# The expert loop of a two-block transformer kernel: spread rows, gather and turning in another order

## The reference, cut to what matters

```python
D_MODEL, N_EXPERTS, TOP_K, D_EXPERT = 1024, 32, 4, 1024
SWIGLU_LIMIT, SWIGLU_ALPHA = 7.0, 1.702

def _expert_ffn(xb, w_gu, b_gu, w_down, b_down):
    gu = xb @ w_gu + b_gu
    gate, up = gu[:, :D_EXPERT], gu[:, D_EXPERT:]
    gate = jnp.minimum(gate, SWIGLU_LIMIT)
    up = jnp.clip(up, -SWIGLU_LIMIT, SWIGLU_LIMIT)
    glu = gate * jax.nn.sigmoid(SWIGLU_ALPHA * gate)
    return ((up + 1.0) * glu) @ w_down + b_down

def moe(xf, router_w, router_b, w_gu, b_gu, w_down, b_down):
    logits = (xf @ router_w + router_b).astype(F32)
    top_val, top_idx = lax.top_k(logits, TOP_K)
    gate = jax.nn.softmax(top_val, axis=-1)
...
    ys = lax.map(run_block, (xs, block_e)).reshape(n_slots, -1)
    return jnp.zeros(xf.shape, F32).at[slot_tok].add(ys.astype(F32) * slot_w[:, None])
```

## Time and profile before

| | us |
|---|---|
| median of 3 runs | 3159.39 (3158.26 to 3159.98) |
| the profiled execution | 3160.19 |
| its span | 3158.3 |
| TensorE busy in the span | 2995.8 (95%) |
| VectorE, ScalarE busy | 842.7, 376.8 |
| share of the chain of waits on L302, all products with weights | 76% |
| the expert stage | from about 659 to 1627 |

### The profile page before, as it was taken

The page is one execution under the profiler, slowest core; times in us unless marked ns, Lnnn a source line. Parts: engine busy times, 40 slices in busy tenths (PEclk is TensorE's granted clock), DMA queues, the critical chain, the costliest instruction groups (busy, mean ns, idle before and its releaser), DMA issues.

```text
span 3158.3 us, 35752 instructions
## 1 busy us (share of the span) xinstructions
PE 2995.8 (95%) x14810; PEld 1952.2 (62%) x14811; DVE 842.7 (27%) x1939; ACT 376.8 (12%) x817; POOL 27.7 (1%) x55
## 2 busy tenths in 40 slices
PE   8989889989999999999989999999999999989999
PEld 6867678833333333333338886675788888756888
DVE  2536341222222222222232103543211111133210
ACT  2122230100000000000010001121000000012000
POOL 0000000000000000000000000000000000000000
PEclk9999999989999999999989999898999999986999
DMA  5122234459999999999963333220243334321340
GB/s 193 53 90 97 80 120 157 187 227 412 425 422 425 421 422 424 422 424 426 421 284 134 133 137 141 81 107 35 107 152 142 133 133 155 133 80 54 133 160 14
DMA packets 49501, 654.86 MB, mean 207 GB/s; under 512 B 5825, under 2 KB 8017, under 8 KB 10193
## 3 DMA queue, kind: packets, MB, share of 16 engines
q1 hardware_dynamic: 45248, 642.90, 51.1%
q0 software_dynamic: 3104, 9.32, 0.9%
q10 hardware_dynamic: 1040, 1.05, 0.1%
HBM read 652.19 MB, written 1.05 MB: 207 GB/s over the span
## 4 chain that ended last, share of the span: by engine, by line
PE 92%; DVE 4%; ACT 2%; issue 1%; DMA 1%; POOL 0%; PEldq 0%; DVEq 0%; PEld 0%; SPq 0%; ACTq 0%; POOLq 0%
PE bank L302 76%; PE bank L2070 2%; PE bank L1087 2%; PE bank L2042 2%; PE bank L2434 1%; PE bank L2443 1%; PE bank L2452 1%; DVE expert_x_slots L2174 1%; PE bank L2048 1%; ACT expert_y_slots L2116 1%; PE bank L2300 1%; PE bank L2838 1%; PE bank L1339 1%; PE bank L2853 0%; PE bank L733 0%
## 5 line engine op out<-in xcount | busy, mean ns | idle before, releaser
L302 PE MATMUL bank<-ffn_x_gained,weight_ring 128*128 128x272 f32 (+1 forms) x2816 | 641.0, 390 | 9.3 <-DVE ffn_x_gained L2317 9.3
L302 PEld LDWEIGHTS bank<-ffn_x_gained,weight_ring 128*128 128x128 f32 x2816 | 536.5, 191 | 112.6 <-DVE ffn_x_gained L2317 11.0
L302 PE MATMUL bank<-weight_ring,expert_x_slots_t 128*64 128x512 f32 x2048 | 457.6, 600 | 0.0
L302 PE MATMUL bank<-x,first_weight_ring 128*128 128x256 f32 x1376 | 323.3, 392 | 29.1 <-DMA first_weight_ring<-weight_stream 12.8
L302 PEld LDWEIGHTS bank<-weight_ring,expert_x_slots_t 128*64 128x64 f32 x2048 | 142.3, 138 | 312.5 <-issue 312.5
L302 PE MATMUL bank<-ffn_h,weight_ring 128*128 128x272 f32 (+1 forms) x1408 | 322.0, 389 | 2.1 <-DVE ffn_up L2396 2.1
L302 PEld LDWEIGHTS bank<-x,first_weight_ring 128*128 128x128 f32 x1376 | 266.4, 196 | 73.2 <-issue 23.9
L302 PEld LDWEIGHTS bank<-ffn_h,weight_ring 128*128 128x128 f32 x1408 | 267.2, 190 | 54.0 <-DVE ffn_up L2396 3.8
L302 PE MATMUL bank<-weight_ring,expert_hidden_slots_t 128*64 128x512 f32 x1024 | 226.8, 595 | 0.0
L302 PE MATMUL bank<-even_hn,weight_ring 128*128 128x272 f32 x656 | 163.9, 406 | 4.4 <-DVE even_hn L2334 4.4
L2179 DVE TENSOR_TENSOR moe_rows<-moe_rows,bank 128x512 f32<-128x512 f32 x128 | 79.4, 682 | 330.9 <-PE bank L2070 330.9
(11 more groups left out here) (572 smaller groups left out, 2374.9 us busy)
## 6 DMA issues: line engine op xcount, KB each, us to landing
weight_ring<-weight_stream SPq DMA_DIRECT2D x276, 2048.0 KB, 9.9
first_weight_ring<-weight_stream SPq DMA_DIRECT2D x30, 2048.0 KB, 7.7
x<-x_t SPq DMA_DIRECT2D x1, 1024.0 KB, 5.9
out_t<-x ACTq DMA_DIRECT2D x1, 1024.0 KB, 4.7
c_ret_ret_q<-const_ret_q POOLq DMA_DIRECT2D x1, 544.0 KB, 5.1
c_ret_ret_k<-const_ret_k POOLq DMA_DIRECT2D x1, 544.0 KB, 5.7
c_odd_pool_inv<-const_pool_inv POOLq DMA_DIRECT2D x1, 544.0 KB, 3.6
c_hgrn_hgrn_levels<-const_hgrn_levels POOLq DMA_DIRECT2D x1, 512.0 KB, 3.8
```

Of the source, the lines that this page charges most:

```text
L302: ins = K.nc.tensor.matmul(out, lhsT, rhs, start=start, stop=stop)
```

## The change

In the short path the spread rows are turned into bank 0 instead of bank 2, behind one more wait of TensorE, for VectorE's reading of the gate products (`gate_read`, a second reader of `gate_sb`). The gather is cut by halves of the tokens: the first half stays before the turning of the activations, the second goes behind it. The next tokens are turned behind the down products instead of before them, into bank 3, and ScalarE copies them to `xt` behind its copy of the down products instead of before. VectorE takes the spread rows from bank 0. In the long path the operations stay in their order, with the added wait.

```diff
+        gate_read = gate_sb.reader()
...
-            def gather_next(pe):
-
-                pe.wait_ge(*pick_ready.take())
-                for b in range(2):
-                    for g in range(2):
-                        ins = nc.tensor.matmul(bank[3][rows[g], :], pick[:, b, :], K.x_rows[:, b, g * HW:(g + 1) * HW], start=b == 0, stop=b == 1)
-                ins.then_inc(*gathered.post())
+            def gather_next(pe, b):
+
+                if b == 0:
+                    pe.wait_ge(*pick_ready.take())
+                for g in range(2):
+                    ins = nc.tensor.matmul(bank[3][rows[g], :], pick[:, b, :], K.x_rows[:, b, g * HW:(g + 1) * HW], start=b == 0, stop=b == 1)
+                if b == 1:
+                    ins.then_inc(*gathered.post())
...
                 pe.wait_ge(*spread_ready.take())
+                pe.wait_ge(*gate_read.take())
                 for b in range(2):
-                    nc.tensor.transpose(bank[2][:, b * P:(b + 1) * P], spread[:, b, :, :].rearrange("p a s -> p (a s)"), eye)
-                gather_next(pe)
+                    nc.tensor.transpose(bank[0][:, b * P:(b + 1) * P], spread[:, b, :, :].rearrange("p a s -> p (a s)"), eye)
+                gather_next(pe, 0)
                 pe.wait_ge(*h_ready.take())
                 for j in range(4):
                     ins = nc.tensor.transpose(bank[5][:, j * P:(j + 1) * P], h[:, 0, j * P:(j + 1) * P], eye)
                 ins.then_inc(*ht_ready.post())
-                turn_next(pe)
+                gather_next(pe, 1)
                 pe.wait_ge(*ht_sb.take())
                 few_linear(pe, bank[2], ht_few, None, y_ready)
+                turn_next(pe, 3)
                 pe.wait_ge(*ys_sb.take())
...
                 act.activation(flat(ht_few[:, :, :]), bank[5][:, :], ACT.Copy).then_inc(*ht_sb.post())
-                copy_next(act)
                 act.wait_ge(*y_ready.take())
                 act.activation(ys[:, :], bank[2][:, :], ACT.Copy).then_inc(*ys_sb.post())
+                copy_next(act, 3)
...
-                dve.tensor_copy(spread_t[:, :], bank[2][:, 0:T])
+                dve.tensor_copy(spread_t[:, :], bank[0][:, 0:T])
```

More of the change, by code:

```diff
@@ L2035, in _, with turn_next @@
             eye = K.con["eye"][:, :]
-            def gather_next(pe):
-                pe.wait_ge(*pick_ready.take())
-                for b in range(2):
-                    for g in range(2):
-                        ins = nc.tensor.matmul(bank[3][rows[g], :], pick[:, b, :], K.x_rows[:, b, g * HW:(g + 1) * HW], start=b == 0, stop=b == 1)
-                ins.then_inc(*gathered.post())
-            def turn_next(pe):
+            def gather_next(pe, b):
[5 more added lines that the diff above has]
+                    ins.then_inc(*gathered.post())
+            def turn_next(pe, at):
                 pe.wait_ge(*xs_sb.take())
                 for j in range(4):
-                    ins = nc.tensor.transpose(bank[4][:, j * P:(j + 1) * P], xs[:, j * P:(j + 1) * P], eye)
+                    ins = nc.tensor.transpose(bank[at][:, j * P:(j + 1) * P], xs[:, j * P:(j + 1) * P], eye)
                 ins.then_inc(*xt_ready.post())
@@ L2078, in many @@
                 many_linear(pe, 4, lambda k: K.x[:, k, 0:T], D, up_ready)
+                pe.wait_ge(*gate_read.take())
                 pe.wait_ge(*h_ready.take())
-                gather_next(pe)
-                turn_next(pe)
+                gather_next(pe, 0)
+                gather_next(pe, 1)
+                turn_next(pe, 4)
                 for b in range(2):
@@ L2089, in many @@
                 pe.nop().then_inc(*out_ready.post())
[L2091 removed]
+            taken = [(sel_ready, 1), (xs_sb, 1), (xt_sb, 1), (spread_ready, 1), (pick_ready, 1), (gate_read, 1), (h_ready, 1), (ht_sb, 1), (ys_sb, 1)]
             posted = [gathered, xt_ready, gate_ready, up_ready, ht_ready, y_ready, out_ready]
@@ L2104, in _, with copy_next @@
         def _(act):
-            def copy_next(act):
+            def copy_next(act, at):
                 act.wait_ge(*xt_ready.take())
-                act.activation(flat(xt[:, :, :]), bank[4][:, :], ACT.Copy).then_inc(*xt_sb.post())
+                act.activation(flat(xt[:, :, :]), bank[at][:, :], ACT.Copy).then_inc(*xt_sb.post())
             def few(act):
@@ L2120, in many @@
                 act.activation(flat(sg[:, :, :]), flat(gate[:, :, :]), ACT.Sigmoid, scale=1.702).then_inc(*sig_ready.post())
-                copy_next(act)
+                copy_next(act, 4)
                 act.wait_ge(*ht_ready.take())
```

## The result

| | us | ratio to before, 95% interval |
|---|---|---|
| before, 4 runs | 3159.68 | |
| changed, 4 runs | 3132.88 (3132.02 to 3137.22) | 0.9918 (0.9901 to 0.9935) |
| changed, once more, 4 runs | 3131.81 | 0.992 (0.9904 to 0.9937) |
| profiled execution, before and changed | 3160.19, 3133.48 | |

The change brings 26.8 us, 0.8%. The forecast was 14.0 us, 3145.4; the measured time lies a tenth of a microsecond under the range's low end of 3133.0. The direction and the saving on TensorE were right. The pace of the stream of weights, which limited the forecast, was wrong.

What follows compares the result with a forecast made beforehand. TensorE was taken as the bound, 29.76 us an expert against the weight stream's 29.70; stored lead 12.6, last expert 0.9 and earlier stream start 0.5 gave 14.0 us, so 3145.4 us, range 3133 to 3149.

Steps and rivals of the forecast that it cites:

- TensorE is the bound before, by a little: Expert stage: TensorE takes 29.76 us an expert, the weight stream 29.70, so TensorE bounds by 0.06 us per expert.
- 0.91 us saved on TensorE: New order from spread rows to output products: TensorE saves 0.91 us per expert, 0.56 at the lower bound, needing 28.85.
- The turning hidden in the wait for ScalarE, at 0: Next tokens turned behind the down products, inside the wait for ScalarE's copy: extra cost 0, upper bound 0.35 us.
- A full 0.53 for the added change: Rule against the sum: each change of shape costs 0.53 us; 0.38 of 0.91 us left, 12.2 of 14.0 in all.
- The stream needs 29.70 us an expert: Expert stage: the weight stream, working without pause, delivers an expert's weights in 29.70 us, at 423 GB/s.
- the lead: Time from an expert's fourth transfer landing to first use: 10.9 to 12.6 us, used up after 12 to 14 experts.
- Sum by the right figure: Whole-kernel gain: 12.6 us of stored lead, 0.9 in the last expert, 0.5 from the stream's earlier start: 14.0 us.
- The earlier start of the stream: Second and third expert's releases come up to 0.9 us sooner each: 0.5 us gained, bounds 0 and 2.
- The stream is faster than these rows say: Rival, expert stage: at 428 GB/s the gain is 22.4 us, 3137.0; with no stream limit 29.1, 3130.3; chance 0.20.
- The clock rival: Rival: TensorE's clock falls on the new waits for weights from about the 14th expert, up to 3193 us; chance 0.05.
- Eaten part: Rival: drains or other waits leave 0.20 to 0.40 us saved per expert, 6 to 13 us in all; chance 0.12.
- exchange: Rival: turning the activations isn't released before 1165.2; below 0.2 us per expert, under 6 us gained, 3155; chance 0.08.

## Why the prediction was half right, point by point

- **TensorE is the bound before, by a little.** Right, but the little is 29.76 - 29.37 = 0.39 us per expert, not 0.06.
- **0.91 us saved on TensorE.** Right: 0.90, and each of its steps as written. The idle 0.2 that now stands ahead of the turned activations is in the sum too: there the gather's first half ends some 0.2 us before 1164.66.
- **The turning hidden in the wait for ScalarE, at 0.** Right. The Trainium skill's rule (TensorEngine Tiling (Array Packing), Key Properties) that changing the tiling mode drains TensorE is neither borne out nor contradicted here: the output products start 0.77 after the turnings do, and whatever a drain takes lies inside the wait. A full 0.53 for the added change, which would have left 0.38 of the saving, did not come.
- **The stream needs 29.70 us an expert.** This is the step that failed. It rested on two readings. "None was as quick as a lone one, so the stream never pauses": wrong, landing times of 7.9 us and more don't exclude pauses; the trace has a step of 31.0 between two fourth transfers, where a steady stream makes 29.4. And "in 28 experts the lead grew by 1.7": true of the end points, but the lead is held between 10.4 and 12.6 us by the ring, so its trend says nothing about the pace. Pauses made up the difference between 29.37 and 29.70: 9.2 us in these 28 experts, most of it in eight pauses of 0.4 to 1.6 us.
- **Sum by the right figure.** The lead falls by 29.37 - 28.86 = 0.51 per expert instead of 0.85. From 10.8 us it lasts 21 experts: the first wait for weights is at the 25th (the 26th in the other run), not the 14th. Against the kernel before, the last expert's fourth transfer is used at 1580.6 instead of 1605.9, 25.3 us sooner; 12.6 of that is the lead, as in the prediction, and 12.7 the transfer's own earlier landing (1580.56 for 1593.3), where the prediction had 0.5, with a bound of 2. The fourth expert's fourth transfer already lands 3.6 us sooner, 747.9 + 10.2 = 758.1 for 761.7; the other 9.1 are the pauses that are gone. With the last expert's 0.9 that is 26.2. The remaining half microsecond lies behind the stage.
- **The earlier start of the stream.** Mis-sized: 3.6 us where the sum had 0.5, which it put in without a price for the jump behind the first expert. From the first to the second expert's output products it is 37.08 us now and was 39.51, 2.43 less. Of these 0.90 are the new order. As an estimate from the rows, 0.6 are a shorter idle stretch of TensorE (5.45 for 6.08) and 0.9 a shorter stretch at the lower clock, which ended at about 701.5 instead of 704.3. The stretch from 703 to 704 before, the first products behind the jump now, and the same stretch now:

```profile
703.00:704.00 1.00, 1.00 (x5) 0.24 (x3) 0.00 (x0) 0.00 (x0) 0.00 (x0) 0.50 0.75 295
```

```profile
695.91 1.97 PE L302 MATMUL bank<-expert_b_gu,expert_select 32*64 32x512 f32 x4 [5.45 <-issue]
```

```profile
703.00:704.00 1.00, 1.00 (x8) 0.32 (x6) 0.00 (x0) 0.00 (x0) 0.00 (x0) 1.00 1.03 442
```

Whether the change causes these 1.5 us is not shown. Taken over each kernel's own pace, this turn costs 9.75 us before, 8.22 now and 8.34 in the changed kernel's second trace; in the other kernels, but for the one with half of the products, it is 8.8 to 9.6. There is one trace of before.
- **The rivals.** "The stream is faster than these rows say" was the case that came, with a chance of 0.20; its first price, 22.4 us, took its pace from the fastest stretch of 30 us, 428 GB/s. That was nearly the right pace (29.41 for 29.37, about 1 us over the stage), but the price kept the 0.5 for the stream's start, 3 us too little; so it is 4 us short. The Trainium skill's ceiling (DMA: Bandwidth & Descriptors, Where 436 GB/s comes from), 435 GB/s, is not reached over a whole stage in any run here: 429 is the most, also with a reader that always waits. The clock rival: it falls, but at waits of 3 us, four in an expert, not at one of 0.3 to 1.3.
- **Eaten part and exchange.** Neither came. The gather behind in one piece, at 3158.39 us, shows what an exchange looks like: the activations are turned sooner, and the down products start no sooner.

What stays open: what each pause of the stream is. They come in the kernels in which TensorE asks for less than 429 GB/s, and once little is queued: in the steady stage of before, each of the eight comes ahead of the landing of a transfer that was issued when the one in front of it had at most 4.7 us to its own. But transfers issued with as little queued, down to 3.0 us, landed without one too. It wasn't tried to tell these apart.

## What to carry to other kernels

A producer behind a ring of buffers runs at its reader's pace, so its mean rate is a lower bound of what it can do, not the rate. Look for its steady stretches, how far apart the landings are when nothing pauses, and take that. And a filler pays only where a wait is: two short waits of one engine need two small fillers, cut to size, while one big one behind the first wait brought nothing here; the order of two copies on the engine waited for decided over as much.

## What the runs showed of the hardware

- The stream of 2 MB transfers from HBM into SBUF on one queue has a steady pace of 4.895 us each, 428 to 429 GB/s, in every kernel of these in which TensorE asked for as much. Transfers of 1 MB take 2.486 us each, 422 GB/s.
- The busy share of the DMA engines is 1.00 to 1.01 at 411, 423 and 429 GB/s alike.
- TensorE's granted clock stayed at 1.00 with one wait for weights of up to 1.3 us per expert, and was 0.89 in the mean with four of up to 3.0 us. Behind the idle 5.45 us after the first expert it was 0.50, the level of 1.2 GHz, for some 5.6 us; behind the idle 6.08 before, for some 7.4.
- Output products (64 rows, 128 columns) start 0.77 us after four turnings of 128 x 128 do, no later than ScalarE's copy lets them.
